# Constants, first modulation and first norm of a transformer trunk in one stage, with the modulation applied per channel after the transpose

## The reference

```
def rms_norm(x, g):
    xf = x.astype(jnp.float32)
    y = xf * lax.rsqrt(jnp.mean(xf * xf, axis=-1, keepdims=True) + RMS_EPS)
    return (y * g.astype(jnp.float32)).astype(x.dtype)

def modulate(h, shift, scale):
    return h * (1 + scale) + shift

silu_c = jax.nn.silu(c)
silu_cc = jax.nn.silu(c_ctx)
# layer i, ada_w[i] is 1024 x 6144
mx = jnp.split((silu_c @ ada_w[i] + ada_b[i])[:, None, :], 6, axis=-1)
mc = jnp.split((silu_cc @ ada_w[i] + ada_b[i])[None, None, :], 6, axis=-1)
hx = modulate(rms_norm(x, norm_mix_pre[i]), mx[0], mx[1])
hc = modulate(rms_norm(ctx, norm_mix_pre[i]), mc[0], mc[1])
# hx and hc then go through the mixer's projection, h @ w_in
```

## Time and profile before

| | |
|---|---|
| time, median of 3 runs | 3670.74 us (3669.35 to 3677.72) |
| time of the profiled execution | 3671.48 us |
| its span, first to last instruction | 3669.4 us |
| TensorE busy | 3313.6 us (90%) |
| VectorE busy | 1857.5 us (51%) |
| ScalarE busy | 1141.4 us (31%) |
| mean granted TensorE clock | 0.954 of full |

### The profile page before, as it was taken

How to read it: one execution, slowest core, us unless ns; L and a number is a source line. 1 busy time by engine, 2 the same in 40 slices (tenths; PEclk the granted TensorE clock), 3 DMA queues, 4 the chain that set the end, 5 groups by cost and what they waited for, 6 DMA issues and landing times. The chain is left out here.

```text
span 3669.4 us, 47554 instructions
## 1 busy us (share of the span) xinstructions
PE 3313.6 (90%) x18952; PEld 2776.3 (76%) x18952; DVE 1857.5 (51%) x2106; ACT 1141.4 (31%) x1843; POOL 295.1 (8%) x525
## 2 busy tenths in 40 slices
PE   3999599796999999999939698999999799999998
PEld 1787477585888888888829577888887588888886
DVE  4599666454344434444445324555554544444446
ACT  2112155456211111111124323555554222122122
POOL 1000000111000000000013111111111100000001
PEclk6999799898999999999969899999999899999999
DMA  4323587332111111111042653322212211111113
GB/s 180 83 81 102 163 262 245 116 115 74 58 46 34 34 34 34 40 40 34 12 163 92 238 171 112 93 56 59 56 44 75 70 58 46 57 44 58 35 46 115
DMA packets 272601, 318.89 MB, mean 87 GB/s; under 512 B 78704, under 2 KB 217552, under 8 KB 271424
## 3 DMA queue, kind: packets, MB, share of 16 engines
q1 hardware_dynamic: 259680, 269.69, 24.4%
q0 software_dynamic: 12768, 47.08, 3.4%
HBM read 246.15 MB, written 70.58 MB: 86 GB/s over the span
## 5 line engine op out<-in xcount | busy, mean ns | idle before, releaser
L1063 DVE TENSOR_TENSOR y_sum<-ffn_down_ps,y_sum 128x512 f32<-128x512 f32 x396 | 271.3, 691 | 242.3 <-PE ffn_down_ps L90 240.3
L88 PE MATMUL ffn_gate_ps<-y_hi,ffn_w_hi 128*128 128x512 f32 (+1 forms) x880 | 326.0, 370 | 36.5 <-DVE ffn_w_lo L1019 36.5
L88 PE MATMUL ffn_down_ps<-ffn_w_hi,ffn_act_hi 128*128 128x512 f32 x792 | 312.0, 394 | 16.8 <-DVE y_sum L1063 10.4
L89 PE MATMUL ffn_gate_ps<-y_lo,ffn_w_hi 128*128 128x512 f32 (+1 forms) x880 | 325.7, 370 | 0.0
L90 PE MATMUL ffn_gate_ps<-y_hi,ffn_w_lo 128*128 128x512 f32 (+1 forms) x880 | 325.3, 370 | 0.0
L89 PE MATMUL ffn_val_ps<-y_lo,ffn_w_hi 128*128 128x512 f32 (+1 forms) x880 | 323.9, 368 | 0.0
L88 PE MATMUL ffn_val_ps<-y_hi,ffn_w_hi 128*128 128x512 f32 (+1 forms) x880 | 323.8, 368 | 0.0
L90 PE MATMUL ffn_val_ps<-y_hi,ffn_w_lo 128*128 128x512 f32 (+1 forms) x880 | 323.7, 368 | 0.0
L89 PE MATMUL ffn_down_ps<-ffn_w_lo,ffn_act_hi 128*128 128x512 f32 x792 | 309.2, 390 | 0.0
L90 PE MATMUL ffn_down_ps<-ffn_w_hi,ffn_act_lo 128*128 128x512 f32 x792 | 308.7, 390 | 0.0
L1019 DVE TENSOR_TENSOR ffn_w_lo<-ffn_raw,ffn_w_hi 128x1024 fp32r<-128x1024 f32 x132 | 158.0, 1224 | 281.0 <-ACT ffn_w_hi L978 280.8
(11 more groups left out here) (292 smaller groups left out, 7017.3 us busy)
## 6 DMA issues: line engine op xcount, KB each, us to landing
ffn_raw<-in_ffn_w_up SPq DMA_DIRECT2D x88, 512.0 KB, 3.8
da_ada_w<-in_ada_w SPq DMA_DIRECT2D x10, 4096.0 KB, 24.8
ffn_raw<-in_ffn_w_down SPq DMA_DIRECT2D x44, 512.0 KB, 5.5
ab_raw<-in_ab_w_in SPq DMA_DIRECT2D x20, 512.0 KB, 3.8
mod_ada_w<-in_ada_w SPq DMA_DIRECT2D x4, 2048.0 KB, 11.2
scratch_mla_q_hi<-up_out_hi POOLq DMA_DIRECT2D x12, 512.0 KB, 2.9
scratch_mla_q_lo<-up_out_lo POOLq DMA_DIRECT2D x12, 512.0 KB, 3.2
scratch_qk_hi<-ab_qk_hi POOLq DMA_DIRECT2D x8, 640.0 KB, 3.2
```

The source lines that it names most:

```text
L88: pe.matmul(out, a_hi, b_hi, start=first, stop=False)
L89: pe.matmul(out, a_hi, b_lo, start=False, stop=False)
L1063: dve.tensor_tensor(part, down_ps[:, half, :], part, ALU.add).then_inc(s.sum_done, 1)
```

## The change

The three stages become one, a new `first_norm`. `first_modulation` and `load_constants` go away, `TokenTail` stays for the later norms.

- The modulation is computed as columns: blocks of `ada_w` (128 channels by 128 columns) are the stationary operand, and the two SiLU vectors are streamed past (two columns). `ada_w` comes in eight pieces of 1 MB: all eight channel blocks by 256 columns, in runs of 1 KB, through a ring of four. Each piece takes 16 matmuls. The result lies in PSUM as [128 channels, 16 blocks, 2 vectors].
- Bias and gain are loaded as columns as well (element by element, `column`), and DVE makes the two sets of columns, shift and (1 + scale) times gain, in two small operations. Nothing is stored to `mod` or loaded from it.
- Token tiles are only multiplied by their reciprocal root (`norm`), transposed (`turn`), and copied from PSUM to a float32 tile `h`, half by DVE (`low_copy`) and half by ACT (`high_copy`). PSUM holds two tiles in flight.
- On TensorE and in SP's queue, a weight piece and a token tile alternate.
- After the last tile, scale and shift are applied in place on `h`, per channel block over all 1280 tokens: four blocks on DVE (`tensor_scalar`), four on ACT (`Identity` with a scale and bias column), two instructions each since the two kinds of token have their own columns. ACT then rounds each of the eight blocks to `h_hi`, and DVE subtracts for `h_lo`.
- Two of the three constant matrices are loaded last.

```diff
-def first_modulation(nc, silu, mod, c, c_ctx, ada_w, ada_b, groups):
...
-def load_constants(nc, consts, ident, turn_a, turn_c):
...
-def first_norm(nc, h_hi, h_lo, x, ctx_rows, pre, ident):
...
+def first_norm(nc, h_hi, h_lo, silu, consts, squares, c, c_ctx, ada_w, ada_b, gain, x, ctx_rows):
+    ident = consts[0]
+    PIECE = 2 * P
+    PIECES = 2 * D // PIECE
+    RING = 4
+    PER_PIECE = PIECE // P
+    SS, MS, RSTD = range(3)
+        def sb(label, shape, dt=F32):
+            return ctx.enter_context(nc.sbuf_tensor(f"norm_{label}", shape, dt))
+        cond = sb("cond", [P, 2, KD])
+        ada = sb("ada", [P, RING, KD, PIECE])
+        bias = sb("bias", [P, 2 * KD])
+        gain_col = sb("gain", [P, KD])
+        cols = sb("cols", [P, 2, KD, 2])
+        x_t = sb("x", [P, RING, D])
+        xn = sb("xn", [P, 2, D])
+        junk = sb("junk", [P, D])
+        h = sb("h", [P, KD, T])
+        small = sb("small", [P, 3, TT])
+        minus_half = sb("minus_half", [P, 1])
+        mod_ps = ctx.enter_context(nc.psum_tensor("norm_mod_ps", [P, 2 * KD, 2], F32))
+        turned = ctx.enter_context(nc.psum_tensor("norm_turned", [P, 2, 2, BANK], F32))
+        s = ctx.enter_context(stage(nc, "norm", [
+            "const_in", "cond_in", "small_in", "ada0_in", "ada1_in", "ada2_in", "ada3_in", "x0_in", "x1_in", "x2_in",
+            "x3_in", "silu_clear", "silu_done", "half_set", "mod_read", "cols_step", "cols_done", "square", "ms_done",
+            "rstd", "xn_done", "turned", "low_copied", "high_copied", "h_vector", "h_scalar", "h_hi", "h_lo"]))
+        ada_in = [s.ada0_in, s.ada1_in, s.ada2_in, s.ada3_in]
+        x_in = [s.x0_in, s.x1_in, s.x2_in, s.x3_in]
+        def tokens(t):
+            return slice(t * P, (t + 1) * P)
+        def parts():
+            return ((slice(0, SEQ), 0), (slice(SEQ, T), 1))
+            def weights(n):
+                if n >= RING:
+                    sp.wait_ge(s.mod_read.sem, n - RING + 1)
+                sp.dma_start(ada[:, n % RING, :, :],
+                             ada_w.rearrange("(k p) n -> p k n", p=P)[:, :, n * PIECE:(n + 1) * PIECE])\
+                  .then_inc(ada_in[n % RING].sem, 16)
+            def rows(t):
+                if t >= RING:
+                    sp.wait_ge(s.xn_done.sem, t - RING + 1)
+                src = x[tokens(t), :] if t < XT else ctx_rows[tokens(t - XT), :]
+                sp.dma_start(x_t[:, t % RING, :], src).then_inc(x_in[t % RING].sem, 16)
+            for r, vec in enumerate((c, c_ctx)):
+                sp.dma_start(cond[:, r, :], column(vec), allow_slow_non_contiguous=True).then_inc(s.cond_in.sem, 16)
+            weights(0)
+            sp.dma_start(ident[:, :], squares[:, 0:P]).then_inc(s.const_in.sem, 16)
+            rows(0)
+            weights(1)
+            rows(1)
+            weights(2)
+            rows(2)
+            weights(3)
+            rows(3)
+            sp.dma_start(bias[:, :], column(ada_b), allow_slow_non_contiguous=True).then_inc(s.small_in.sem, 16)
+            sp.dma_start(gain_col[:, :], column(gain), allow_slow_non_contiguous=True).then_inc(s.small_in.sem, 16)
+            for n in range(RING, PIECES):
+                weights(n)
+                rows(n)
+            for t in range(PIECES, TT):
+                rows(t)
+            for j, m in enumerate(consts[1:]):
+                sp.dma_start(m[:, :], squares[:, (j + 1) * P:(j + 2) * P]).then_inc(s.const_in.sem, 16)
+            sp.wait_ge(s.const_in.sem, 48)
+        @block.tensor
+        def _(pe):
+            def modulation(n):
+                pe.wait_ge(ada_in[n % RING].sem, 16 * (n // RING + 1))
+                for j in range(PER_PIECE):
+                    for k in range(KD):
+                        mm = pe.matmul(mod_ps[:, n * PER_PIECE + j, :], ada[:, n % RING, k, j * P:(j + 1) * P],
+                                       silu[:, k, 0:2], start=k == 0, stop=k == KD - 1)
+                mm.then_inc(s.mod_read.sem, 1)
+            def turn(t):
+                pe.wait_ge(s.xn_done.sem, t + 1)
+                if t >= 2:
+                    pe.wait_ge(s.low_copied.sem, t - 1)
+                    pe.wait_ge(s.high_copied.sem, t - 1)
+                for k in range(KD):
+                    mm = pe.transpose(turned[:, t % 2, k // 4, k % 4 * P:(k % 4 + 1) * P],
+                                      xn[:, t % 2, k * P:(k + 1) * P], ident[:, :])
+                mm.then_inc(s.turned.sem, 1)
+            pe.wait_ge(s.silu_done.sem, 1)
+            for n in range(PIECES):
+                modulation(n)
+                if n == 0:
+                    pe.wait_ge(s.const_in.sem, 16)
+                turn(n)
+            for t in range(PIECES, TT):
+                turn(t)
+            def square(t):
+                act.wait_ge(x_in[t % RING].sem, 16 * (t // RING + 1))
+                if t:
+                    act.wait_ge(s.square.sem, t)
+                act.activation(junk[:, :], x_t[:, t % RING, :], ACT.Square, accum_out=small[:, SS, t:t + 1])\
+                   .then_inc(s.square.sem, 1)
+            def high_copy(t):
+                act.wait_ge(s.turned.sem, t + 1)
+                act.activation(h[:, 4:KD, tokens(t)], turned[:, t % 2, 1, :].rearrange("p (k n) -> p k n", n=P),
+                               ACT.Copy).then_inc(s.high_copied.sem, 1)
+            def modulated(k):
+                for at, r in parts():
+                    ins = act.activation(h[:, k, at], h[:, k, at], ACT.Identity, scale=cols[:, 1, k, r:r + 1],
+                                         bias=cols[:, 0, k, r:r + 1])
+                ins.then_inc(s.h_scalar.sem, 1)
+            def rounded(k):
+                if k % 2:
+                    act.wait_ge(s.h_scalar.sem, k // 2 + 1)
+                else:
+                    act.wait_ge(s.h_vector.sem, k // 2 + 1)
+                act.activation(h_hi[:, k, :], h[:, k, :], ACT.Copy).then_inc(s.h_hi.sem, 1)
+            act.wait_ge(s.cond_in.sem, 32)
+            act.wait_ge(s.silu_clear.sem, 1)
+            act.activation(silu[:, :, 0:2], cond[:, :, :].rearrange("p r k -> p k r"), ACT.Silu)\
+               .then_inc(s.silu_done.sem, 1)
+                    square(t)
+                if t:
+                    high_copy(t - 1)
+            act.wait_ge(s.low_copied.sem, TT)
+            act.wait_ge(s.high_copied.sem, TT)
+            act.wait_ge(s.cols_done.sem, 1)
+            for k in range(1, KD, 2):
+                modulated(k)
+                rounded(k - 1)
+                rounded(k)
+            def norm(t):
+                dve.wait_ge(s.rstd.sem, t + 1)
+                if t >= 2:
+                    dve.wait_ge(s.turned.sem, t - 1)
+                dve.tensor_scalar(xn[:, t % 2, :], x_t[:, t % RING, :], small[:, RSTD, t:t + 1], None, ALU.mult)\
+                   .then_inc(s.xn_done.sem, 1)
+            def low_copy(t):
+                dve.wait_ge(s.turned.sem, t + 1)
+                dve.tensor_copy(h[:, 0:4, tokens(t)], turned[:, t % 2, 0, :].rearrange("p (k n) -> p k n", n=P))\
+                   .then_inc(s.low_copied.sem, 1)
+            def columns():
+                dve.wait_ge(s.mod_read.sem, PIECES)
+                dve.wait_ge(s.small_in.sem, 32)
+                dve.tensor_tensor(cols[:, :, :, :].rearrange("p a k r -> p (a k) r"), mod_ps[:, :, :],
+                                  bias[:, :].rearrange("p (a b) -> p a b", b=1).broadcast_to([P, 2 * KD, 2]), ALU.add)\
+                   .then_inc(s.cols_step.sem, 1)
+                dve.wait_ge(s.cols_step.sem, 1)
+                dve.scalar_tensor_tensor(out=cols[:, 1, :, :], in0=cols[:, 1, :, :], scalar=1.0,
+                                         in1=gain_col[:, :].rearrange("p (a b) -> p a b", b=1).broadcast_to([P, KD, 2]),
+                                         op0=ALU.add, op1=ALU.mult).then_inc(s.cols_done.sem, 1)
+            def modulated(k):
+                for at, r in parts():
+                    ins = dve.tensor_scalar(h[:, k, at], h[:, k, at], cols[:, 1, k, r:r + 1], cols[:, 0, k, r:r + 1],
+                                            ALU.mult, ALU.add)
+                ins.then_inc(s.h_vector.sem, 1)
+            def rest(k):
+                dve.wait_ge(s.h_hi.sem, k + 1)
+                dve.tensor_tensor(h_lo[:, k, :], h[:, k, :], h_hi[:, k, :].bitcast(F32), ALU.subtract)\
+                   .then_inc(s.h_lo.sem, 1)
+            dve.memset(silu[:, :, :], 0.0).then_inc(s.silu_clear.sem, 1)
+                    norm(t)
+                if t:
+                    low_copy(t - 1)
+                if t == PIECES:
+                    columns()
+            dve.wait_ge(s.low_copied.sem, TT)
+            dve.wait_ge(s.high_copied.sem, TT)
+            dve.wait_ge(s.cols_done.sem, 1)
+            modulated(0)
+            for k in range(0, KD, 2):
+                if k + 2 < KD:
+                    modulated(k + 2)
+                rest(k)
+                rest(k + 1)
```

(72 more changed lines are left out.)

17 lines of the change are left out of this document (removed).

## The result

Over 20 runs each, the changed kernel's median is 3679.85 us (3675.12 to 3684.70) against 3674.28 us (3668.79 to 3678.17) before: a ratio of 1.0017, 95% interval 1.0010 to 1.0023. That is 5.6 us more, clear of noise and under the 0.2% that the prediction called no change. The profiled execution took 3675.12 us (span 3673.3) against 3671.48 (3669.4). It is the shortest of the 20 of the changed kernel, and that of the kernel before is 2.8 us under its median.

A forecast was written before the change was run, and what follows sets the result against it. TensorE bounds the whole span; the change touches the serial first 96 us. At the low clock: first piece 8.2, eight steps of 8.6, copies 81.9, tail 17.8, next stage 100.5, +4.5: 3675 us (3672 to 3680; 8 in 10: 3643 to 3681).

The forecast's parts named there:

- First piece at 8.2: Start of the modulation: the first 1 MB weight piece is there at 8.2 us (7.6 to 9.3).
- A piece of 6.9 us and a step of 8.6 at the lower clock: TensorE in the modulation: 16 matmuls at 0.43 us a piece, with a tile's transposes at 1.7 us, eight such steps.
- PE waits for nothing between the pieces; transfers hide: Modulation loop: 4.4 us of transfers for a piece and tile stay behind TensorE's 8.6 us; each root is ready in time.
- Last tile's copies at 81.9: End of the tiles: eighth tile transposed at 77.0, last tile's product at 79.2, its transposes at 81.1, copies at 81.9.
- Tail 17.8 us: Scale, shift, rounding and subtraction over all tokens after the last copies: 17.8 us, bounds 17.5 and 19.
- Rival 3: In the tail, ACT's alternation of Identity and Copy loads up to eight tables: +10 us, 3685; chance 0.07.
- Next stage at 100.5: The projection's start: last instruction ends at 99.7, 0.8 us later the next stage starts, instead of 96.03: +4.5 us.
- What would show it: Signs in the profile after: 256 matmul records, granted clock 0.50 from 10 to 80 us, tail 17.8 us without table load.
- Rival 1: TensorE's clock opens in the modulation: a step of 4.3 us, -26 us, 3644; chance 0.28.
- Rival 2: The clock opens for only some modulation steps; with half of them full, -17 us from the forecast, 3658; chance 0.09.
- the likeliest range: Whole kernel with the low clock throughout: 3672 to 3680 us around 3675; chance 0.56.
- the wide one: Whole kernel, range of 8 in 10, reaching into the open clock: 3643 to 3681 us.

The follow-up runs named there:

- experiment 2: Changed kernel with 32 columns streamed for each weight square instead of 2, the extra ones zeros, results unchanged; one run, 3680.79 us.
- Experiment 1: Changed kernel with every other channel block left out of the modulation, 8 instead of 16 matmuls a piece, output incomplete; one run, 3658.3 us.
- experiment 6: Changed kernel with SiLU vectors stationary and weights streamed, bias and gain loaded behind the last tile; 3641.89 us, ratio 0.9923 to the kernel before.
- experiment 3: Changed kernel with 128 columns streamed for each weight square, the 32 repeated four times, results unchanged; 3654.56 us, ratio 0.9947 to the kernel before.
- experiment 4: Changed kernel with four dummy matmuls of 512 columns while TensorE waits for the first weight piece, results unchanged; one run, 3676.64 us.
- experiment 5: Changed kernel with SiLU vectors stationary, 512 weight columns streamed, finished rows turned into columns by four transposes; 3646.36 us, ratio 0.9929 to the kernel before.

## Why the prediction was right

It was right in its direction, in its size and in the mechanism that decided: TensorE at the lower clock set the pace, and the result is a small loss, under what it called no change. It gave +4.5 us; the two traces show +3.9, the medians +5.6 (the interval is 3.7 to 8.5 us). Some terms came out by errors that cancel, and they are named below.

- *First piece at 8.2.* Measured 8.25.
- *A piece of 6.9 us and a step of 8.6 at the lower clock.* Measured 6.83 and 25.24 - 16.81 = 8.43. The one-column matmuls of a later stage were a good stand-in, though they stream half the columns: the number of columns does not set the time, as experiment 2 shows with 32 columns at the same price, and PE's weight loads are busy for all of it (10.00 of 10.00 us).
- *PE waits for nothing between the pieces; transfers hide.* So it was. Transfers ran at the pace forecast as well: the squares of the first tiles start at 9.62, 13.91 and 18.23 in the changed kernel, 4.3 us apart, where the sum said 4.4. Experiment 1 shows that they did not set the pace. The price of the element-wise columns (0.9 us for 1000) was read from a row of `conv_b`, the small load queued behind such a load and not that load itself. In the changed kernel the issue of the gain column held SP's queue for 7.25 us, which TensorE's work hid; experiment 6 gives 3.0 us for what was priced at 2.8.
- *Last tile's copies at 81.9.* Measured 81.25. This is three errors that nearly cancel. The eighth tile was transposed at about 75.8, 1.2 us sooner than the 77.0 of the sum. Then the last tile's product ended at 79.37 (78.62 + 0.75), 3.6 us later instead of 2.2. The sum said that DVE's order decides here; but ACT squares the last tile only after its copy of tile 7 (76.54), GpSimd makes the root, and DVE waits 1.58 us for it. Last, the tile's transposes ran at the full clock, 1.10 us and not 1.7 + 0.25.
- *Tail 17.8 us.* From 81.29 to 98.94, 17.65: ACT's chain of sixteen instructions and one subtraction. Here too two errors cancel: a pair of ACT's multiply-adds took 82.93 - 81.29 = 1.64 us, not 1.45, and a rounding (85.25 - 82.93) / 2 = 1.16, not 1.27. DVE's multiply-add took 0.81 us for 1024 tokens, near the 0.75 taken and not the 1.2 of the upper bound; the whole tail has no table load. Rival 3, that alternating the two ACT functions would cost, is out.
- *Next stage at 100.5.* Measured 99.90, 0.96 after the last instruction where 0.80 was taken.
- *What would show it.* The 256 records are there. The clock column was misjudged: I said that it would read 0.50, and that 1.00 with pieces of 3.4 us would speak for the first rival. It reads 1.00 with pieces of 6.83, because nothing is recorded before the rise at 77.3 us; the durations decide.

The deciding choice was the lower clock, and it was a choice between two readings, not a result of rows: the trace before had no uninterrupted stretch of such matmuls. It was given a chance of 0.56, so part of the success is luck. The trace after shows that the choice was right, and experiments 2 to 4 show what it hangs on: with the same weight loads, 128 columns opened the clock, and 2 or 32 did not. That all 20 runs of the changed kernel lie within 9.6 us says the same of each of them, since an open clock is worth some 25 us (experiment 3). Rival 1, the opened clock, was priced at -26 us from the kernel before with the next stage at 68.6 to 70; with 128 columns it started at 71.89, 24.1 us earlier than before, and the median was 19.5 us lower. In the two profiled executions the rest of the kernel took 8.3 us longer with 128 columns (the table's last column); why is open. For this stage the rival's sum was sound, 2 to 3 us short, and its condition was not met. Rival 2, a clock open in some of the steps, is out as well: all eight pieces took 6.83 to 6.96 us. The Trainium skill (TensorE: Matmul & The Clock Gate, "Why this matters for your kernels") says that a TensorE kept busy gets the full clock. By that rule this rival would have been the forecast. But PE was busy from 8.25 us without a break, and all eight pieces up to 74.06 ran at the lower clock. The measurement decides: in this kernel being busy with weight loads was not enough.

The level, 3675 us, was further off: the change landed at 3679.85, just inside the upper end of the likeliest range (3680) and 1.2 us inside that of the wide one (3681). 3.5 us of that come from the kernel before, whose median was 3670.74 over 3 runs and 3674.28 over 20. That the level stayed in the range is luck in part; the difference of the two kernels is what was forecast well.

The gain that the change could have had was lost in one place. It removed 22.0 us of round trip, 4.7 us of a stage of its own and DVE's bound of 4.1 us a tile, and it turned a product that kept TensorE busy for 12.7 us in all (four bursts like those of the earlier trace rows) into one of 54.7. With the products the old way round (experiments 5 and 6) the same change is worth 0.7 to 0.8% of the kernel before.

## What to carry to other kernels

A float32 matrix-vector product with the matrix as the stationary operand paid a full weight load for each 128x128 square here, 0.43 us with 2 to 32 columns at the lower clock and 0.22 with 2 or 128 at the full one; with the vector stationary and the matrix streamed in column groups the same 8.4 MB took a quarter of TensorE's time, and four transposes (0.7 us) turn the rows into columns afterwards. Before a change makes an engine the only one that works, ask which clock it will have there: if the weight loads must stay, try 128 columns in place of two, since they cost nothing at the full clock and kept it open here. Where transfers set the pace, element-wise columns belong behind the large loads of a queue, not between them: 3.0 us here.

## What the runs showed of the hardware

- A plain float32 matmul of a 128x128 square takes 0.43 us at the lower clock with 2 and with 32 columns (pieces of 6.83 and 6.87 us). At the full clock it takes 0.22 with 2 columns (experiment 4) and with 128 (experiment 3, start to start).
- TensorE, busy without a gap for 66 us (8.25 to 74.06) on two-column matmuls and runs of eight transposes, stayed at the lower clock. With 128 columns the clock opened within the first piece (6.07 us, rise recorded at 13.0 us). After four matmuls of 512 columns it was open for part of the next piece (4.66 us), and then fell (10.6 us) although the engine never idled.
- Sixteen transposes in a row (3.50 us at 74.06) were followed by eight at the full clock (1.10 us at 79.43) after an idle of 1.9 us, and the trace records the rise at 77.3, near the end of the sixteen; the same in experiments 1 and 4, not in experiment 2 (1.97 us). So long runs of transposes may open the clock; no run tells them apart from the matmuls ahead of them. The Trainium skill (TensorE: Matmul & The Clock Gate, "Part 4: PE-mode transpose") says that transposes don't count as busy in the same way. Experiment 2 and the norm before agree with it, the other three kernels speak against it.
- A 1 MB piece in runs of 1 KB with a 0.5 MB tile came every 4.3 us (the changed kernel); with runs of 8 KB in the piece, every 3.77 us (experiments 5 and 6).
